# Hybrid attention: values evicted two steps late, masks two ahead, unread products on TensorE, first scores ahead of the last z half

## The chip, the cores and the metric

The kernel is one program on one core of a Trainium2 chip. The metric is the device time of the whole program in microseconds (us): the median of several executions. Beside the times there is one execution recorded by the hardware profiler. Engines are named as in the profile: PE (TensorE's matmuls), PEld (its weight loads, which overlap the matmuls), DVE (VectorE), ACT (ScalarE), POOL (GpSimd), and SP, which here only issues DMAs.

## What is computed

A long network on one sequence of 256 tokens of width 1024. First two blocks (a recurrent mixer with a feed-forward part, then differential attention with eight experts), then two layers of hybrid attention. The change touches only the last part, which in the reference is:

```python
def hybrid_layer(x, c, positions, ...):          # twice: l = 0, 1
    ...
    h = rms_norm_2(x, norm_g) * (1 + scale) + shift
    z = h @ w_in                                  # 1024 -> 2976
    c_q, c_kv, k_rope, g_mla, q_b, k_b, v_b, g_moba = jnp.split(z, ...)
    o_mla  = mla_attention(...)                   # 8 heads, q and k of width 96, v of 64, causal
    o_moba = moba_attention(...)                  # 8 heads of width 64, causal, with a bias by distance
    y = jnp.concatenate([silu(g_mla) * o_mla, silu(g_moba) * o_moba], -1) @ w_out
    return x + gate * y
```

With 256 tokens the blocks of moba are one block, so both attentions are a causal softmax over 256 keys.

## The kernel before

Every engine has its own instruction list, written out by hand; engines meet at semaphores. The eight PSUM banks are given out by a plan (`make_plan`, L162): each use of a bank has a name, an order, a bank and the engine that empties it ("a" ACT, "v" DVE, "e" the exponentials on ACT). `fill` on PE waits until the bank's use before has been emptied, `take` waits until PE has filled it, `wait_taken` waits until it has been emptied. DVE and ACT wait for each of their own instructions before the next one.

Large products run in fp32r as three passes (high times high, low times high, high times low; L1139 to L1141), from weights that ACT (`high`, L2824) and DVE (`low`, L1896) split into a high and a low part after their DMA. A half of a weight tile is one `high` and one `low`.

A hybrid layer on PE: the z chunks in the order 0, 2, 3, 4, 1, 5 (`by_token`, two halves j = 0, 1 each), between them small products and transposes. Between the halves of z chunk 5, `mla_heads` transposes the mla queries and keys (L1746). Then come 16 attention steps: i = 0 to 7 are moba, i = 8 to 15 mla; a step handles two heads (g) and one half of the queries (m = i mod 2), so even steps have 128 keys and odd ones 256. After the loop come the output products (`out_product`, L1803).

A step i passes over the engines like this:

- PE `scores(i)` (L1759; L1763 and L1764 for mla), into two alternating sets of banks by i mod 2. The bank for step i + 2 is free when ACT has finished `exponentials(i)`.
- DVE `masked(i)`: bias or mask (L2706, L2708), row maximum (L2711), for mla one tiny product more (L2714).
- ACT `exponentials(i)`: two activations, each followed by a read of the sum's accumulator (L3227).
- DVE `sums_inverted(i)`: one reciprocal (L2719), after the exponentials of i.
- PE `weights_transposed(i)`: 2 or 4 transposes (L1774), after the exponentials of i; ACT `weights_out(i)` copies them out (L3238).
- PE `values(i)`: the product with v (L1787); DVE `values_out(i)` scales it into O2 (L2726).

The orders of the three lists in the loop are: PE `scores(i+2)`, `weights_transposed(i)`, `values(i-1)`; DVE `masked(i+1)`, `sums_inverted(i)`, `values_out(i-1)`; ACT `exponentials(i+1)`, `weights_out(i)`. Into the loop are put: two `high` on ACT (after steps 2 and 3), two `low` on DVE (after steps 4 and 5), `heads_gated` (L2731) for the moba half on DVE after step 8, and at step 10 the transposes of that half on PE (`gated_to_channels`, L1797) with their copies on ACT (L2809) and DVE (L1916). A PE matmul of fp32 operands shows as two records, one of fp32r as one.

XTH is the fp32r tile that holds the high part of the layer's input during the z chunks and of the gated output later; its first two slices are next written after the loop.

Of the kernel before, what the change touches and what calls it, by code (L numbers as in the profile page):

```python
# [22 lines left out]
P = 128  # L23
# [100 lines left out]
class Plan:  # L124
# [7 lines left out]
    def add(self, name, who, bank=None):  # L132
        self.index[name] = len(self.by)
        self.bank.append(len(self.by) % 8 if bank is None else bank)
        self.by.append(who)
# [26 lines left out]
def make_plan():  # L162
# [141 lines left out]
    for l in range(DEPTH2):  # L304
        for u in range(4):
            add((("h", l), "xT", u), "v", 4 + u)

        def z_chunk(c):
            for m in range(TT):
                add(("z", l, c, m), "a" if c in (1, 5) else "av"[m], 2 * (Z_ORDER.index(c) % 2) + m)  # L310

        def pair_scores(i):
            for c in range(1 if i >= 8 else 2):
                add(("pair", l, "scores", i, c), "e", 2 * (i % 2) + c)

        z_chunk(0)
        if l == 0:
            for u in range(2):
                add(("mod_gate", 1, u), "v", 6 + u)
        z_chunk(2)  # L320
        for u in range(2):
            add(("cT", l, u), "a", 4 + u)
        z_chunk(3)
        for c in range(4):
            for m in range(TT):
                add(("up", l, c, m), "av"[m], 4 + (2 * c + m) % 4)
        z_chunk(4)
        z_chunk(1)
        for u in range(4):
            add(("mobaT", l, u), "av"[u % 2], 4 + u)  # L330
        for u in range(8):
            add(("mlaT", l, u), "av"[u % 2], 4 + u % 4)
        z_chunk(5)
        pair_scores(0)
        pair_scores(1)
        for i in range(17):
            if i < 14:
                pair_scores(i + 2)
            if i == 10:
                for u in (2, 3):  # L340
                    add(("yT", l, u), "v", 2 * u - 3)
            if i < 16:
                add(("pair", l, "weightsT", i), "a", 4 + i % 2)
            if i:
                add(("pair", l, "values", i - 1), "v", 6 + (i - 1) % 2)
        for u in range(2):
            add(("yT", l, u), "v", 4 + u)
        for c in range(2):
            for m in range(TT):
                add(("w_out", l, c, m), "v", 2 * m + 1 - c)  # L350
# [152 lines left out]
def build(nc, I, consts, buckets, out):  # L503
# [4 lines left out]
    with ctx:  # L508
# [155 lines left out]
        def fill(pe, name):  # L664

            i = PLAN.index[name]
            before = PLAN.emptied_before(i)
            if before is not None:
                pe.wait_ge(emptied[before[0]], before[1])
            return banks[PLAN.bank[i]]  # L670
# [6 lines left out]
        def wait_taken(eng, name):  # L677

            i = PLAN.index[name]
            who = PLAN.by[i]  # L680
            eng.wait_ge(emptied[who], sum(w == who for w in PLAN.by[:i + 1]))
# [422 lines left out]
        def _(pe):  # L1104
            mm = nc.tensor.matmul
# [405 lines left out]
            def scores(i):  # L1511

                h, m = DIFF_STEPS[i]
                w = (m + 1) * P
                qk = QKT[h // 4]
                b = [fill(pe, ("diff", "scores", i, c)) for c in range(2)]
                for c in range(2):
                    r = slice(64 * c, 64 * c + 64)
                    mm(b[c][:, 0:w], qk[r, h % 4, m * P:(m + 1) * P], qk[r, 4 + h % 4, 0:w],
                       start=True, stop=True).then_inc(filled, 1)  # L1520

            def weights_transposed(i):

                m = DIFF_STEPS[i][1]
                b = fill(pe, ("diff", "weightsT", i))
                pe.wait_ge(weights, i + 1)
                for k in range(m + 1):
                    last = nc.tensor.transpose(b[:, k * P:(k + 1) * P], AT[:, i % 2, k * P:(k + 1) * P], IDENT)
                last.then_inc(filled, 1)
# [204 lines left out]
            for l in range(DEPTH2):  # L1734
# [6 lines left out]
                def mla_heads(j):  # L1741

                    if j == 0:
                        return
                    pe.wait_ge(mla_ready, l + 1)
                    to_channels(("mlaT", l), 8, lambda u: [  # L1746
                        (96, (2 * i + m) * P, QK[:, m, (2 * u + i) * 96:(2 * u + i + 1) * 96])
                        for i in range(2) for m in range(TT)])

                def scores(i):  # L1750

# [12 lines left out]
                    mm(b[:, T:T + w], QKT2[0:96, 2 * g + 1, q], QKT2[0:96, 9 + 2 * g, 0:w],  # L1764
                       start=True, stop=True).then_inc(filled, 1)

                def weights_transposed(i):

                    m = PAIR_STEPS[i % 8][1]
                    b = fill(pe, ("pair", l, "weightsT", i))  # L1770
                    pe.wait_ge(exps, 16 + 16 * l + i + 1)
                    for c in range(2):
                        for k in range(m + 1):
                            last = nc.tensor.transpose(b[:, (2 * c + k) * P:(2 * c + k + 1) * P],  # L1774
                                                       EE2[:, i % 2, c, k * P:(k + 1) * P], IDENT)
                    last.then_inc(filled, 1)
# [62 lines left out]
                    (P, (2 * j + m) * P, ZB[:, m, ZQ + (2 * u + j) * P:ZQ + (2 * u + j + 1) * P])  # L1839
                    for j in range(2) for m in range(TT)])  # L1840
                z_chunk(5, mla_heads)
                wait_taken(pe, ("mobaT", l, 2))
                wait_taken(pe, ("mobaT", l, 3))
                scores(0)
                scores(1)
                for i in range(17):
                    if i == 6:
                        wait_taken(pe, ("mlaT", l, 6))
                        wait_taken(pe, ("mlaT", l, 7))
                    if i < 14:  # L1850
                        scores(i + 2)
                    if i == 10:
                        gated_to_channels((2, 3))
                    if i < 16:
                        weights_transposed(i)
                    if i:
                        values(i - 1)
                wait_taken(pe, ("yT", l, 3))
# [9 lines left out]
        def _(v):  # L1868
# [746 lines left out]
            for l in range(DEPTH2):  # L2615
# [112 lines left out]
                def heads_gated(at, z, c):  # L2728

                    wait_taken(v, ("z", l, c, 1))  # L2730
                    V(tt_(O2[:, :, at:at + 512], O2[:, :, at:at + 512], ZB[:, :, z:z + 512], MUL), o_ready)  # L2731
# [26 lines left out]
                for u in range(1, 8, 2):  # L2758
                    b = take(v, ("mlaT", l, u)).rearrange("p (g t) -> p g t", g=2)
                    V(ts(QKT2[0:96, 2 * u:2 * u + 2, :], b[0:96], prm("mla_columns", 2 * l + u // 4)[0:96], None, MUL), ev)  # L2760
                masked(0)
                for i in range(16):
                    if i < 15:
                        masked(i + 1)
                    sums_inverted(i)
                    if i == 10:
                        x_out(("yT", l), units=(2, 3))
                    if i:
                        values_out(i - 1)
                    if i in (4, 5):  # L2770
                        low()
                    elif i == 8:
                        heads_gated(512, ZGB, 5)
                values_out(15)
                heads_gated(0, ZG, 1)
                x_out(("yT", l), units=(0, 1))
# [555 lines left out]
```

## Time and profile before

| | us |
|---|---|
| median of 3 executions (2017.39 to 2021.28) | 2018.95 |
| the profiled execution | 2015.8 |
| its span, first to last instruction | 2014.0 |

The page of the profile gives busy time by engine, the span in 40 slices with the clock that was granted to TensorE (tenths of full speed; 1.0 is 2.4 GHz, 0.5 is 1.2 GHz), and the chain of work that ended last. The trace behind it can be asked for any stretch: busy time of each engine and the granted clock (windows), instructions in order of time (timeline), who waited for whom (waits), and the chain in order of time. In the timeline "[2.42 <-X]" says that the engine was idle for 2.42 us before the row, and what released it. Rows of one line that follow each other are merged: start, duration, and the count behind the shape. PE's matmuls are pipelined, so the cost of one is read from start to start, not from its duration.

The 16 steps of layer 0 lie between 1745.77 and 1802.42 us of the span, those of layer 1 between 1923.78 and 1983.19 us.

### The profile page before, as it was taken

To read this page: it belongs to the slowest core of one execution; us is meant where nothing else is said; L and a number is where in the kernel's file an instruction comes from. 1 tells how busy PE (TensorE), PEld (TensorE's weight loads), DVE (VectorE), ACT (ScalarE), POOL (GpSimd) and SP (SyncE) were. 2 spreads that over 40 slices of the span, in tenths; PEclk is the share of its full clock that TensorE was granted. 3 is DMA by queue.
4 is the path that set the end of the run, shared out by engine and by line. 5 is a ranking of instruction groups with operands and counts; after the bars stand their busy time and mean duration, and the time that the engine had idled before them with its cause. 6 is when DMAs were issued, how large, how long until landed. Compare 5 with 4: busy or idle time off the path is not lost.

```text
span 2014.0 us, 25785 instructions
## 1 busy us (share of the span) xinstructions
PE 1886.5 (94%) x9376; PEld 1580.4 (78%) x9376; DVE 1561.2 (78%) x1532; ACT 1163.4 (58%) x1218; POOL 59.8 (3%) x85
## 2 busy tenths in 40 slices
PE   7989999999877999999999999999999989888987
PEld 7888678887756788888888888888888877677766
DVE  5877768887674789898897888888888976656754
ACT  5632344435473667677676776686766755545452
POOL 2000011111100000000000000000000000000000
PEclk9999899999967999999999999999999999879968
DMA  6301269995412899999999999999999954214410
GB/s 222 126 1 43 80 239 318 332 308 176 136 42 106 298 380 331 374 347 362 371 339 371 350 361 368 341 372 347 363 345 358 378 175 152 84 43 138 153 62 22
DMA packets 161948, 489.03 MB, mean 243 GB/s; under 512 B 8178, under 2 KB 13427, under 8 KB 161744
## 3 DMA queue, kind: packets, MB, share of 16 engines
q1 hardware_dynamic: 153536, 458.21, 62.6%
q0 software_dynamic: 8336, 29.81, 4.2%
q8 instruction: 48, 0.79, 0.2%
q14 instruction: 28, 0.23, 0.0%
HBM read 485.36 MB, written 2.62 MB: 242 GB/s over the span
## 4 chain that ended last, share of the span: by engine, by line
PE 66%; DVE 14%; issue 10%; DMA 4%; ACT 4%; POOL 0%; DVEq 0%; ACTq 0%; POOLq 0%
PE bank L1139 19%; PE bank L1141 18%; PE bank L1140 18%; DVE weights_at L1896 4%; PE bank L1630 2%; DMA BIG<-in_e_ffn_down 2%; ACT weights_at L2824 2%; DVE BIG L2241 2%; PE bank L1348 1%; PE bank L1695 1%; PE bank L1336 1%; DMA BIG<-in_e_ffn_up 1%; DMA BIG<-in_e_w_in 1%; DMA BIG<-in_w_ada 1%; PE bank L1374 1%
## 5 line engine op out<-in xcount | busy, mean ns | idle before, releaser
L2482 DVE TENSOR_TENSOR expert_weights_low<-BIG,expert_weights_high 128x2048 fp32r<-128x2048 f32 x336 | 750.4, 2288 | 56.9 <-ACT expert_weights_high L3107 56.4
L3107 ACT ACTIVATE expert_weights_high<-BIG 128x2048 fp32r<-128x2048 f32 x336 | 625.0, 1922 | 65.1 <-DMA BIG<-in_o_moe_up 38.5
L1139 PE MATMUL bank<-expert_weights_high,expert_x_high 128*128 128x512 f32 x896 | 352.4, 393 | 2.4 <-DVE expert_x_low L2547 2.3
L1141 PE MATMUL bank<-expert_weights_low,expert_x_high 128*128 128x512 f32 x896 | 350.0, 391 | 0.0
L1140 PE MATMUL bank<-expert_weights_high,expert_x_low 128*128 128x512 f32 x896 | 349.7, 390 | 0.0
L1896 DVE TENSOR_TENSOR weights_at<-BIG,weights_at 128x2048 fp32r<-128x2048 f32 (+2 forms) x100 | 219.1, 2191 | 83.0 <-ACT weights_at L2824 80.9
L2824 ACT ACTIVATE weights_at<-BIG 128x2048 fp32r<-128x2048 f32 (+2 forms) x100 | 183.6, 1836 | 167.0 <-DMA BIG<-in_e_ffn_down 42.0
L1139 PE MATMUL bank<-weights_at,x_high 128*128 128x512 f32 (+2 forms) x608 | 244.9, 403 | 22.5 <-DVE weights_at L1896 8.3
L1140 PE MATMUL bank<-weights_at,x_low 128*128 128x512 f32 (+2 forms) x608 | 239.7, 394 | 0.0
L1141 PE MATMUL bank<-weights_at,x_high 128*128 128x512 f32 (+2 forms) x608 | 239.6, 394 | 0.0
L1139 PEld LDWEIGHTS bank<-expert_weights_high,expert_x_high 128*128 128x128 f32 x896 | 168.8, 188 | 36.8 <-DVE expert_x_low L2547 2.4
L1141 PEld LDWEIGHTS bank<-expert_weights_low,expert_x_high 128*128 128x128 f32 x896 | 168.5, 188 | 35.1
L1140 PEld LDWEIGHTS bank<-expert_weights_high,expert_x_low 128*128 128x128 f32 x896 | 168.8, 188 | 34.1
L1139 PE MATMUL bank<-expert_weights_high,expert_hidden_high 128*128 128x512 f32 x448 | 176.1, 393 | 0.0
L1141 PE MATMUL bank<-expert_weights_low,expert_hidden_high 128*128 128x512 f32 x448 | 174.7, 390 | 0.0
L1140 PE MATMUL bank<-expert_weights_high,expert_hidden_low 128*128 128x512 f32 x448 | 174.4, 389 | 0.0
L1139 PEld LDWEIGHTS bank<-weights_at,x_high 128*128 128x128 f32 x608 | 118.1, 194 | 50.3 <-issue 9.8
L1141 PEld LDWEIGHTS bank<-weights_at,x_high 128*128 128x128 f32 x608 | 117.4, 193 | 25.3
L1140 PEld LDWEIGHTS bank<-weights_at,x_low 128*128 128x128 f32 x608 | 118.1, 194 | 24.0 <-issue 0.5
L3154 ACT ACTIVATE expert_hidden_high<-bank 128x512 fp32r<-128x512 f32 x56 | 30.9, 596 | 168.8 <-PE bank L1695 168.8
L1141 PEld LDWEIGHTS bank<-expert_weights_low,expert_hidden_high 128*128 128x128 f32 x448 | 84.1, 188 | 17.8
L1140 PEld LDWEIGHTS bank<-expert_weights_high,expert_hidden_low 128*128 128x128 f32 x448 | 84.2, 188 | 17.1
(400 smaller groups left out, 2350.3 us busy)
## 6 DMA issues: line engine op xcount, KB each, us to landing
BIG<-in_o_moe_gate SPq DMA_DIRECT2D x112, 1024.0 KB, 5.1
BIG<-in_o_moe_up SPq DMA_DIRECT2D x112, 1024.0 KB, 5.3
BIG<-in_o_moe_down SPq DMA_DIRECT2D x112, 1024.0 KB, 5.0
BIG<-in_w_ada POOLq DMA_DIRECT2D x48, 512.0 KB, 4.8
BIG<-in_w_in SPq DMA_DIRECT2D x20, 1024.0 KB, 5.0
BIG<-in_o_w_qkv SPq DMA_DIRECT2D x12, 1024.0 KB, 5.0
BIG<-in_e_w_in SPq DMA_DIRECT2D x10, 1024.0 KB, 5.2
BIG<-in_e_ffn_gate SPq DMA_DIRECT2D x10, 1024.0 KB, 5.4
```

The source lines that it names most:

```text
L1139: mm(b, high_l, high_r, start=start, stop=False, skip_group_check=not check)
L1140: mm(b, low_l, high_r, start=False, stop=False, skip_group_check=not check)
L1141: last = mm(b, high_l, low_r, start=False, stop=stop, skip_group_check=not check)
L1336: last = mm(b[:, i * P:(i + 1) * P], AM[:, 4 * gr + i, :], YI[:, 4 * gr + i, :], start=True, stop=True)
L1348: last = mm(b[:, i * P:(i + 1) * P], lhs[:, k, :], rhs[:, k, :], start=True, stop=True)
L1630: last = mm(b[:, k * P:(k + 1) * P], XN[:, m, d * P:(d + 1) * P], PSEL[:, m, :], start=m == 0, stop=m == TT - 1)
L1896: V(tt_(WM[low_at][:, 0:n_], whole, WM[high_at][:, 0:n_].bitcast(F32), SUB), low_ready)
L2241: V(stt(ADAS[i], w_, s_cc[:, k:k + 1], ADAS[i], MUL, ADD), ada_used)
L2482: tt_(E_WL[q % E_SLOTS], half(q % E_SLOTS), E_WH[q % E_SLOTS].bitcast(F32), SUB).then_inc(w_low, 1)
L2824: A(f(WM[halves.pairs[g][0]][:, 0:whole.shape[1]], whole, ACT.Copy), high_ready)
L3107: f(E_WH[q % E_SLOTS], half(q % E_SLOTS), ACT.Copy).then_inc(w_high, 1)
L3154: f(E_HTH[:, h], b, ACT.Copy).then_inc(xh_high, 1)
```

## The change

Four things are changed, in both hybrid layers. On PE `scores(0)` moves from behind z chunk 5 to between its halves, after the transposes of mla (the plan's order moves with it). On PE a new function `opened(i, n)` takes the bank of step i's transposed weights and runs n fp32r products of 128 columns by 512 into it, which nothing reads and which the transposes overwrite: six at step 0, two at each of steps 1 to 15, ahead of `scores(i+2)`. On DVE `masked` runs two steps ahead instead of one and `values_out` two steps behind instead of one, and the order in a step becomes `values_out(i-2)`, `sums_inverted(i)`, `masked(i+2)`. On DVE `heads_gated` of the moba half goes from step 8 to the end of step 9, and at step 10 `x_out` goes to the end of the step. ACT's list is as before.

```diff
--- before.py
+++ after.py
@@ -330,8 +330,8 @@
             add(("mobaT", l, u), "av"[u % 2], 4 + u)
         for u in range(8):
             add(("mlaT", l, u), "av"[u % 2], 4 + u % 4)
+        pair_scores(0)
         z_chunk(5)
-        pair_scores(0)
         pair_scores(1)
         for i in range(17):
             if i < 14:
@@ -1746,6 +1746,9 @@
                     to_channels(("mlaT", l), 8, lambda u: [
                         (96, (2 * i + m) * P, QK[:, m, (2 * u + i) * 96:(2 * u + i + 1) * 96])
                         for i in range(2) for m in range(TT)])
+                    wait_taken(pe, ("mobaT", l, 2))
+                    wait_taken(pe, ("mobaT", l, 3))
+                    scores(0)
 
                 def scores(i):
 
@@ -1764,10 +1767,16 @@
                     mm(b[:, T:T + w], QKT2[0:96, 2 * g + 1, q], QKT2[0:96, 9 + 2 * g, 0:w],
                        start=True, stop=True).then_inc(filled, 1)
 
-                def weights_transposed(i):
+                def opened(i, full_products):
+
+                    b = fill(pe, ("pair", l, "weightsT", i))
+                    for _ in range(full_products):
+                        mm(b, XTH[:, 0, 0:P], XTH[:, 0:2, :], start=True, stop=True, skip_group_check=True)
+                    return b
+
+                def weights_transposed(i, b):
 
                     m = PAIR_STEPS[i % 8][1]
-                    b = fill(pe, ("pair", l, "weightsT", i))
                     pe.wait_ge(exps, 16 + 16 * l + i + 1)
                     for c in range(2):
                         for k in range(m + 1):
@@ -1839,20 +1848,19 @@
                     (P, (2 * j + m) * P, ZB[:, m, ZQ + (2 * u + j) * P:ZQ + (2 * u + j + 1) * P])
                     for j in range(2) for m in range(TT)])
                 z_chunk(5, mla_heads)
-                wait_taken(pe, ("mobaT", l, 2))
-                wait_taken(pe, ("mobaT", l, 3))
-                scores(0)
                 scores(1)
                 for i in range(17):
                     if i == 6:
                         wait_taken(pe, ("mlaT", l, 6))
                         wait_taken(pe, ("mlaT", l, 7))
+                    if i < 16:
+                        weights_bank = opened(i, 2 if i else 6)
                     if i < 14:
                         scores(i + 2)
                     if i == 10:
                         gated_to_channels((2, 3))
                     if i < 16:
-                        weights_transposed(i)
+                        weights_transposed(i, weights_bank)
                     if i:
                         values(i - 1)
                 wait_taken(pe, ("yT", l, 3))
@@ -2759,18 +2767,20 @@
                     b = take(v, ("mlaT", l, u)).rearrange("p (g t) -> p g t", g=2)
                     V(ts(QKT2[0:96, 2 * u:2 * u + 2, :], b[0:96], prm("mla_columns", 2 * l + u // 4)[0:96], None, MUL), ev)
                 masked(0)
+                masked(1)
                 for i in range(16):
-                    if i < 15:
-                        masked(i + 1)
+                    if i >= 2:
+                        values_out(i - 2)
                     sums_inverted(i)
-                    if i == 10:
-                        x_out(("yT", l), units=(2, 3))
-                    if i:
-                        values_out(i - 1)
+                    if i < 14:
+                        masked(i + 2)
                     if i in (4, 5):
                         low()
-                    elif i == 8:
+                    elif i == 9:
                         heads_gated(512, ZGB, 5)
+                    elif i == 10:
+                        x_out(("yT", l), units=(2, 3))
+                values_out(14)
                 values_out(15)
                 heads_gated(0, ZG, 1)
                 x_out(("yT", l), units=(0, 1))
```

## Rows read from the trace of the kernel before

**Rows 1.** The page: PE's busy time, and the granted clock in 40 slices.
```profile
PE 1886.5 (94%) x9376; PEld 1580.4 (78%) x9376; DVE 1561.2 (78%) x1532; ACT 1163.4 (58%) x1218; POOL 59.8 (3%) x85
PEclk9999899999967999999999999999999999879968
```

**Rows 2.** Windows, both stages: from:to, length, busy us by engine, clock, DMA share.
```profile
1745.77:1802.42 56.65, 44.42 (x217) 37.97 (x217) 32.47 (x76) 32.53 (x86) 0.00 (x0) 0.66 0.11 38
1923.78:1983.19 59.41, 45.63 (x217) 38.57 (x217) 32.44 (x76) 32.54 (x86) 0.00 (x0) 0.65 0.11 36
```

**Rows 3.** Waits in layer 0's stage: us in total, times, longest.
```profile
DVE BIG L2726 <- PE bank L1787: 16.1, 11, 3.3
ACT BIG L3227 <- DVE SM L2714: 7.8, 6, 2.0
```

**Rows 4.** The chain that ended last, in layer 1's stage, one turn: start, us.
```profile
1954.24 0.76 PE bank L1787 x4
1955.10 0.30 DVE BIG L2726
1955.42 0.44 DVE bank L2708
...
1956.86 0.66 ACT BIG L3227 x2
...
1958.30 0.83 PE bank L1763 x2
```

**Rows 5.** Windows around changes of the clock (columns as in rows 2), layer 0.
```profile
1747.40:1749.80 2.40, 0.00 (x0) 0.02 (x1) 1.47 (x3) 2.23 (x6) 0.00 (x0) 1.00 0.00 0
1751.10:1757.06 5.96, 5.96 (x26) 4.78 (x26) 2.23 (x6) 2.79 (x10) 0.00 (x0) 0.50 0.01 3
1774.00:1777.80 3.80, 3.80 (x17) 3.41 (x16) 0.66 (x2) 1.51 (x5) 0.00 (x0) 0.50 0.24 93
1781.00:1782.00 1.00, 1.00 (x7) 0.87 (x6) 0.90 (x4) 0.11 (x1) 0.00 (x0) 0.62 0.00 0
1788.10:1798.50 10.40, 7.12 (x48) 6.00 (x47) 7.22 (x22) 6.22 (x19) 0.00 (x0) 0.99 0.01 2
1736.60:1740.00 3.40, 3.40 (x34) 3.40 (x32) 2.02 (x3) 2.15 (x4) 0.00 (x0) 1.00 0.35 135
```

**Rows 6.** Windows of one pair of steps each: moba at half, mla at half, mla at full clock.
```profile
1932.03:1938.87 6.84, 6.04 (x27) 4.84 (x27) 3.48 (x10) 4.36 (x11) 0.00 (x0) 0.50 0.00 0
1946.76:1954.78 8.02, 6.68 (x26) 6.02 (x27) 4.79 (x9) 3.69 (x11) 0.00 (x0) 0.50 0.69 245
1791.35:1796.12 4.77, 3.85 (x27) 3.36 (x27) 2.74 (x10) 3.39 (x10) 0.00 (x0) 1.00 0.01 3
```

**Rows 7.** Timeline of PE: end of z chunk 5, first scores, first output products, layer 1.
```profile
1923.21 0.40 PE L1140 MATMUL bank<-weights_at,x_low 128*128 128x512 f32 x1
1923.45 0.40 PE L1141 MATMUL bank<-weights_at,x_high 128*128 128x512 f32 x1
1923.78 0.49 PE L1759 MATMUL bank<-BIG 64*128 64x128 f32 x4
1924.68 0.70 PE L1759 MATMUL bank<-BIG 64*128 64x256 f32 x4 [0.41 <-ACT BIG L3208]
1927.81 0.65 PE L1759 MATMUL bank<-BIG 64*128 64x128 f32 x4 [2.42 <-ACTq L3230]
...
1984.62 0.63 PE L1139 MATMUL bank<-weights_at,x_high 128*128 128x512 f32 x1
1985.05 0.63 PE L1140 MATMUL bank<-weights_at,x_low 128*128 128x512 f32 x1
```

**Rows 8.** Timelines of ACT and DVE, layer 1: table load, one high, one low.
```profile
1925.38 1.28 ACT L3227 ACT_TABLE_LOAD   x1 [0.84 <-DVE SM L2711]
...
1935.79 1.91 ACT L2824 ACTIVATE weights_at<-BIG 128x2048 fp32r<-128x2048 f32 x1
...
1942.32 2.29 DVE L1896 TENSOR_TENSOR weights_at<-BIG,weights_at 128x2048 fp32r<-128x2048 f32 x1
```

## The prediction, made before the changed kernel was run

> **What bounds the kernel now.** First the page: PE is busy 94% of the span, so time is to be had only where PE is late or slow, and the clock row shows where: the last two of its dips (slices 35 and 36, then 39 and 40) lie at and after the attention stages of the two hybrid layers [rows 1]. Then the windows of these stages: 56.65 and 59.41 us, PE busy for 44.4 and 45.6 of them, at a mean granted clock of 0.66 and 0.65 [rows 2]. So PE has work for about three quarters of the stage, and much of that runs at 1.2 GHz. Then the waits: the longest is DVE at `values_out`, 16.1 us in 11 waits for PE's `values`; ACT in turn waits 7.8 us for the tiny product that ends `masked` in the mla steps [rows 3]. The chain joins the two: `values(i-1)`, `values_out(i-1)`, mask and maximum of i + 2, exponentials of i + 2, then the next scores on PE [rows 4]. DVE stands at `values_out` while the scores that it is to mask next are there already. So the stage is a loop through all three engines in which none is full, and PE's idle time in it lowers the clock, which makes the loop longer.
>
> **DVE's order.** Afterwards `values_out(i-2)` stands ahead of `sums_inverted(i)`. `values(i-2)` on PE comes before `scores(i+1)`, so it is done by about the time that the exponentials of i end, and `sums_inverted(i)` and `masked(i+2)` need those anyway: the wait of 16.1 us has no successor at this place. What is late next is the loop exponentials(i), scores(i+2), mask(i+2), exponentials(i+2), two steps long. In the mla steps with 256 keys the chain gives 1.44 us for mask, maximum and their signal (1955.42 to 1956.86) and 1.44 for the exponentials and theirs (to 1958.30); the scores of one of the two heads take 0.83 there, mostly at the low clock [rows 4], so I take 1.0 for both at full clock and 0.2 for their signal: 4.1 us in two steps. Against it stand the engines' own sums. DVE: 32.47 less two `low` of 2.29 is 27.9, 3.5 us for each of the eight pairs of steps. ACT: 32.53 less the table load of 1.28 and two `high` of 1.91 is 27.4, or 3.4 a pair [rows 2, 8]. PE: 6.04 at half clock for a moba pair, so 3.0 at full, and 3.85 at full for an mla pair [rows 6].
>
> **The unread products.** An fp32r product of 512 columns costs 0.24 us at full clock (1923.21 to 1923.45) and 0.43 at half (1984.62 to 1985.05) [rows 7]; their weight loads overlap as those of all such products do. A layer has 36: 8.4 us of PE at full clock, 15.5 at half. A pair of steps gets four: PE then needs 4.0 us for a moba pair and 4.8 for an mla pair at full clock, and 7.8 and 8.4 at half. Below zero their direct cost can't go; what they can bring is the clock. At full clock PE becomes the fullest engine of the loop by about half a microsecond a pair. The bank that `opened(i)` takes was emptied by `weights_out(i-2)`, for which `values(i-2)` one step earlier has waited already: no new wait.
>
> **The clock.** It fell from 2.4 to 1.2 GHz after PE had stood still for 2.4 us at the loop's start (2.42 us, released by ACT's exponentials [rows 7]; the same in layer 0 [rows 5]). It rose again after 3.8 us without a gap, 1774.0 to 1777.8; it did not rise in 5.96 us without a gap, 1751.10 to 1757.06, so uninterrupted work is not by itself enough. It fell again at 1781 (0.62), after a gap of 1.3 us, and held at 0.99 for 10.4 us from 1788.1 with PE busy for 7.12 of them, 68% [rows 5]. With the products PE is busy for 80% and more of the stage at full clock (36 us of work in the 44 worked out below), and at half clock it has no gaps at all. I take from this that the clock is mostly 2.4 GHz, with one spell at 1.2 in each layer.
>
> PE's transposes are a point against it. The row: from 1736.6 to 1740.0 PE did nothing but transposes and the clock stayed at 1.00 [rows 5]. The Trainium skill, "TensorE: Matmul & The Clock Gate", Part 4: PE-mode transpose, says that a transpose doesn't count as PE being busy the way a matmul does. By that rule the stage would be worth less to the clock than its busy time says, and the second rival below would be what happens; by the row it would not.
>
> **First scores and the start.** `scores(0)` ahead of the last z half puts 0.35 to 0.5 us in front of that half (its two products take 0.49 us in the timeline [rows 7]; I take 0.42). It lets mask and maximum of step 0 be done early, so that ACT goes from its last z copy straight into the table load: the 0.84 us that it stood idle before the load go [rows 8]. Net -0.4 us a layer, between +0.5 and -0.9. From the last z product to the end of the first exponentials: z copy 0.9, table load 1.3, exponentials 0.9, so 3.1 us. `scores(1)` still waits for that z copy, and the six products (1.4 us) fill over half of the 2.42 us gap behind it.
>
> **The sum for one layer** at full clock, from placing the operations of the three lists one after the other with these durations, zero at the last z product: exponentials end at 3.1 (step 0), 6.0 (2), 11.6 (4), 17.0 (6), 23.1 (8), 26.9 (10), 32.9 (12), 37.8 (14) and 40.7 (15); the last transposes, copy and values take 2.6: 43.3. Of the 34.7 between steps 0 and 14, PE's own sum is four times 4.0 and three times 4.8, 30.4. The 4.3 more are what is not hidden of two `high` (3.8 on ACT, steps 2 and 3), two `low` (4.6 on DVE, steps 4 and 5) and step 10, where gate, transposes and copies follow each other on DVE, PE and ACT. Moved later by a step, gate and `x_out` cost between nothing and 1.2 us more than before, and lie in this sum. SP's loads of the last output weights wait for the two `low`, which come earlier; a load has the rest of the loop, over 20 us. With `scores(0)` 43.7. For one spell at half clock and for signals that I placed too tightly I add 2.3: 46.0 a layer, against 56.65 and 59.41. That is 116.1 less 92.0: **24 us**. Behind the loop the first eight output products run at half clock now (0.43 apart, layer 1 at 1984.6, against 0.24 [rows 7]); if the clock holds, 1.5 us a layer more, which I leave to the range.
>
> The profiled execution took 2015.8 us (span 2014.0); less 24 it would take 1991.8. The median of the runs shown is 3 us above it; I forecast the median: **1995 us**.
>
> **Rivals.**
>
> The period stays where full clock has it today. In the old order at 2.4 GHz the shortest pair took 4.8 us [rows 6], and the stretch from 1788.1 to 1798.5, some two pairs, gives 5.2 each [rows 5]. If semaphore latencies rather than the wait at `values_out` make that, the stage is 3.1 + 7 times 5.2 + 5 + 5.5 = 50, and the saving 116.1 - 100.8 = 15: 2004.
>
> The clock is mixed: a quarter of the stage at 1.2 GHz. All of it at half clock is PE's sum: four times 7.8, four times 8.4, six products, transposes of the gate, and 3.3 to start, near 73 us. A quarter of the way from 46 to 73 is 52.7: the saving is 11, 2008. For it: the fall at 1781 after only 1.3 us of gap. Against: nothing filled gaps then.
>
> Slower: the clock stays down. Then PE is the bound, and every step pays 0.86 us for two products that bring nothing. With the whole loop at 1.2 GHz the stages take 73 each, 30 us more than now: 2049. It decides at a stage of 58 us, that is with some 45% of the loop at half clock. For it: the 5.96 us without a gap and no rise. Against: the rises and the 10.4 us that held.
>
> The change doesn't do what it says: DVE's wait only moves to `sums_inverted`, because ACT's order (exponentials of i + 1 before the copy of i) was the bound all along, and the products fill the idle time. Then 2018 within 0.2%. Against: DVE's 16.1 us are waits for PE, not for ACT [rows 3].
>
> **How the numbers follow.** Forecast 0.58 (1986 to 2001, the low end with the output products and no spell at half clock), old period 0.16, mixed clock 0.13, slower 0.08, no effect 0.05. A measurement of this kernel tells about 0.2%, 4 us, from no change. Range 1985 to 2011: forecast and the first two rivals. Faster 0.87, same 0.05, slower 0.08.
>
> **What would show it.** Right: the wait of DVE at `values_out` for PE nearly gone; the mean clock of both stages over 0.9; no gap of PE over 2 us; a pair of mla steps in 4.6 to 5.0 us; stages of 43 to 49 us. Wrong: a clock near 0.5 with PE busy all through (slower); a clock of 1.0 and pairs of over 5.2 us (the old period); waits of the same size before `sums_inverted`; or a gap that opens behind the loop, so that a shorter stage doesn't shorten the span.

## Result and the profile after

The changed kernel takes 1984.0 us (median of four executions, 1983.4 to 1985.4) against 2018.3 for the kernel before (2017.4 to 2021.3): a ratio of 0.983, with an interval of 0.981 to 0.985. I had forecast 1995 with a range of 1985 to 2011. The sign and the direction of the mechanism were right. The saving, 34 us, was larger than the 24 I forecast, and the time lies 1 us below my range. Two executions in the series below, one of the kernel before and one of the early split, ran at a mean clock of 0.55 and 0.60 and took 3129 and 3173 us; they stand in no ratio.

The page of the changed kernel, lines as in [rows 1]:

```profile
PE 1872.3 (94%) x9448; PEld 1564.1 (79%) x9448; DVE 1561.3 (79%) x1532; ACT 1164.6 (59%) x1218; POOL 59.9 (3%) x85
PEclk9999899999967899999999999999999999999999
```

PE has 72 matmuls more and is busy 14 us less. The two dips at the attention stages (slices 35, 36, 39 and 40 in [rows 1]) are gone.

The two stages as windows, from the start of the last z product to the first output product (columns as in [rows 2]), and three more windows of the same kernel behind them: layer 1's one spell at a lower clock, and two places at the change of layers.

```profile
1744.93:1787.59 42.66, 37.25 (x251) 29.66 (x249) 31.59 (x74) 32.59 (x86) 0.00 (x0) 1.00 0.15 50
1909.55:1952.30 42.75, 38.44 (x251) 31.30 (x249) 31.60 (x74) 32.58 (x86) 0.00 (x0) 0.96 0.15 50
1926.00:1931.00 5.00, 5.00 (x28) 4.66 (x27) 4.53 (x6) 2.91 (x10) 0.00 (x0) 0.66 0.63 211
1815.00:1819.00 4.00, 2.62 (x12) 2.62 (x13) 0.57 (x2) 0.42 (x1) 0.61 (x1) 0.50 0.84 260
1891.00:1895.00 4.00, 2.14 (x5) 1.79 (x6) 3.97 (x2) 0.00 (x0) 0.00 (x0) 0.73 0.25 57
```

[Rows 2] count from the instruction behind that z product, 0.33 us later (1923.45 and 1923.78 in [rows 7]); from its start the stages before took 56.98 and 59.74. All stages below are counted from its start. So the stages became 14.3 and 17.0 us shorter, 31.3 together, and the granted clock rose from 0.66 and 0.65 to 1.00 and 0.96. The whole span went from 2014.0 to 1981.8, 32.2 less. The difference between that and the stages is small: 0.5 gained ahead of the first stage, 0.9 lost between the stages (121.03 to 121.96 us), 1.3 gained behind the second (30.8 to 29.5). The medians differ by 34.3, since the profiled execution of before (2015.8) lay 2.5 below its median.

Four of the waits in layer 0's stage (engine, line, whom it waits for: us in total, times, longest), in the order of the list; rows between them are left out at the dots:

```profile
DVE bank L2714 <- PE bank L1762: 8.6, 6, 6.1
...
ACT BIG L3237 <- DVE SM L2722: 3.5, 4, 2.3
...
DVE BIG L2734 <- PE bank L1796: 1.9, 3, 1.2
...
DVE SM L2727 <- ACT BIG L3237: 0.4, 2, 0.2
```

Lines have moved: `values_out` is L2734 now (L2726 before), `values` L1796, the mask L2714, the exponentials L3237, `sums_inverted` L2727. DVE's wait at `values_out` went from 16.1 us in 11 waits [rows 3] to 1.9 in 3. It didn't move to `sums_inverted` (0.4). ACT's wait for the tiny product ahead of the mla exponentials went from 7.8 to 3.5. DVE's 8.6 us at the mask have one wait of 6.1 in them: that is the start of the stage, where the scores of step 1 stand behind the last z half.

What bounds the loop now can be read from the chain that ended last. One turn of the mla half of layer 1, its longest pieces (start, us, engine, line):

```profile
1940.50 0.84 PE bank L1796 x8
1941.34 0.52 PE bank L1774 x2
1941.86 0.43 PE bank L1766 x2
1942.29 0.43 PE bank L1767 x2
1942.72 0.44 PE bank L1783 x4
```

In [rows 4] the same turn ran PE, DVE, DVE, ACT, PE. Now all of this turn is PE: values, the two unread products (L1774), scores, transposes, each right behind the one before. In the moba half the chain still goes through ACT, and two pieces of it are its `high`, 1.9 us each:

```profile
1916.73 0.57 ACT BIG L3237 x2
1917.33 0.57 ACT BIG L3237 x2
...
1918.49 1.92 ACT weights_at L2834
1920.43 0.47 ACT BIG L3237 x2
1920.92 0.47 ACT BIG L3237 x2
1921.55 0.61 ACT BIG L3248
...
1922.18 1.92 ACT weights_at L2834
```

### The profile page after: what moved, and what is told of

Read it like the earlier page. It is cut to its first block, busy times and chain, and to the rows that moved or that the text cites. A ratio compares the mean times of both kernels' runs of the same rounds, so it can differ in the third digit from the quotient of the medians.

```text
span 1981.8 us, 25897 instructions
## 1 busy us (share of the span) xinstructions
PE 1872.3 (94%) x9448; PEld 1564.1 (79%) x9448; DVE 1561.3 (79%) x1532; ACT 1164.6 (59%) x1218; POOL 59.9 (3%) x85
## 4 chain that ended last, share of the span: by engine, by line
PE 75%; DVE 9%; issue 9%; ACT 3%; DMA 2%; POOL 0%; DVEq 0%; POOLq 0%; ACTq 0%
PE bank L1139 21%; PE bank L1141 21%; PE bank L1140 21%; PE bank L1630 2%; PE bank L1348 2%; DVE weights_at L1904 1%; PE bank L1695 1%; ACT weights_at L2834 1%; PE bank L1336 1%; DMA BIG<-in_e_ffn_gate 1%; PE bank L1433 1%; PE bank L1374 1%; DVE x_low L1931 1%; DMA BIG<-in_e_ffn_up 0%; PE bank L1126 0%
```

## Experiments

The result alone can't say which part did it: DVE's order, the products and `scores(0)` came together, and the clock rose with them. The first four kernels take the change apart. The kernels that follow ask what the clock was worth, how many products are best, what the loop is made of, and whether the two `high` and `low` that stand on the new chain can go elsewhere.

I compare stages from the traces, one profiled execution of each kernel, and not whole times alone: these carry up to 8 us from work ahead of the stage. With the same instructions ahead of it, the last z product of the first stage started anywhere between 1744.9 us (the changed kernel) and 1753.5 (the kernel with one product a step). Each pair of rows below is layer 0 and layer 1, with columns as in [rows 2].

### The change taken apart

**DVE's order alone.** The kernel before, with only the new list on DVE:

```diff
                 masked(0)
+                masked(1)
                 for i in range(16):
-                    if i < 15:
-                        masked(i + 1)
+                    if i >= 2:
+                        values_out(i - 2)
                     sums_inverted(i)
-                    if i:
-                        values_out(i - 1)
+                    if i < 14:
+                        masked(i + 2)
...
+                values_out(14)
                 values_out(15)
```

> Only DVE's order is changed (masks two ahead, values evicted two late, gate and x_out at their new places); no unread products, scores(0) behind z chunk 5 as before. Theory A (order and products are both needed: the order opens the loop, the products keep the clock at 2.4 GHz): the 2.4 us gap of PE at the loop's start is still there, the clock falls, and PE at 1.2 GHz with 6.0 to 6.7 us of work a pair becomes the bound: stages of about 50 us, 16 us saved, 2002 (1996 to 2008), mean clock 0.6 to 0.8. Rival B (the order alone gives it, the products only fill idle time): stages of 43, 1984 to 1988. Rival C (the clock alone gives it): 2016 to 2019.

**The products alone.** DVE's list and `scores(0)` as before, two unread products a step and six at the start on PE:

```diff
+                    if i < 16:
+                        weights_bank = opened(i, 2 if i else 6)
                     if i < 14:
                         scores(i + 2)
```

> Only the unread products are added (six, then two a step); DVE's order and scores(0) as before. Theory A: the clock holds at over 0.9, but the loop through values_out stays, at 4.8 to 5.2 us a pair: stages of about 50 us, 2000 (1994 to 2008). Rival B: the products stand on the path at a low clock and bring nothing: 2018 to 2030. Rival C: 1984 to 1990.

**All but the products.** The changed kernel with none of them:

```diff
-                        weights_bank = opened(i, 2 if i else 6)
+                        weights_bank = opened(i, 0)
```

> The changed kernel without any unread product: new DVE order and scores(0) ahead of the last z half. Theory A: PE stands still for about 1.7 us at the start and again at the two highs and lows; the clock falls for part of the stage: 1990 to 2002, mean clock 0.65 to 0.9. Rival B: 1982 to 1986. Rival C: 2015 to 2018.

**First scores alone.** As the last, and DVE's list as before; of the change only `scores(0)` ahead of the last z half is left:

> Only scores(0) goes ahead of the last z half; DVE's order as before, no products. Theory A, by the prediction's sum: exponentials of step 0 about 0.4 us earlier a layer, 0.8 us in all, so 2017 to 2018; the clock falls at the start as before. Rival: the shorter gap of PE at the start (about 1.7 instead of 2.4 us) keeps the clock up in the first steps: 2005 to 2014.

The stages, in this order (order alone, products alone, all but the products, first scores alone):

```profile
1750.41:1795.71 45.30, 38.08 (x218) 32.03 (x217) 32.46 (x76) 32.57 (x86) 0.00 (x0) 0.77 0.14 47
1915.48:1960.94 45.46, 38.37 (x218) 31.83 (x217) 32.46 (x76) 32.58 (x86) 0.00 (x0) 0.77 0.15 47
...
1743.93:1800.00 56.07, 45.17 (x254) 35.51 (x253) 32.45 (x76) 32.59 (x86) 0.00 (x0) 0.85 0.12 38
1924.14:1980.41 56.27, 45.23 (x254) 35.67 (x253) 32.45 (x76) 32.57 (x86) 0.00 (x0) 0.85 0.11 38
...
1745.02:1789.35 44.33, 36.02 (x214) 30.31 (x213) 31.60 (x74) 32.58 (x86) 0.00 (x0) 0.81 0.15 48
1909.76:1953.52 43.76, 32.67 (x214) 27.24 (x213) 31.61 (x74) 32.57 (x86) 0.00 (x0) 0.88 0.15 49
...
1750.88:1810.79 59.91, 49.77 (x214) 42.91 (x213) 31.59 (x74) 32.54 (x86) 0.00 (x0) 0.57 0.10 36
1932.75:1989.22 56.47, 44.08 (x214) 37.63 (x213) 31.59 (x74) 32.53 (x86) 0.00 (x0) 0.66 0.12 38
```

Both layers together: before 116.7, order alone 90.8, products alone 112.3, all but the products 88.1, first scores alone 116.4, the changed kernel 85.4. The order by itself brings 26.0 of the 31.3 us, at a clock of only 0.77. The products by themselves bring the clock to 0.85, higher than the order does, and the stage stays at 56: 4.4 us. Read down the clock column against the lengths: a stage of 56 at 0.85 and one of 45 at 0.77 can't both be explained by the clock. Neither single kernel came out as I had expected: the order alone took less than the 50 us I had put on it and more than the 43, and the products alone took more than 50, at a clock below 0.9.

The wait says why. At `values_out`, layer 0, first with the order alone, then with the products alone:

```profile
DVE BIG L2726 <- PE bank L1787: 3.8, 5, 1.3
...
DVE BIG L2733 <- PE bank L1792: 15.2, 10, 3.3
```

With the products alone PE is faster, and DVE stands at the same wait nearly as long as before (15.2 us against 16.1).

The order has parts that no kernel here takes apart: the masks two ahead, the values two behind, and the new places of gate and `x_out`. One wait of before prices the last of them. It stands at `x_out` in step 10, once a layer, and with the order alone it is gone:

```profile
DVE x_low L1916 <- ACT x_high L2809: 2.1, 1, 2.1
```

If all of it was on the path, it is 2.1 us of the 11.7 and 14.3 that the order brings in the two layers; the wait at `values_out` fell by 12.3 in layer 0. How the rest divides between the masks and the values is not shown.

On top of the order, the products are worth 2.7 us for both layers (88.1 to 85.4), `scores(0)` 2.7 as well (90.8 to 88.1), but `scores(0)` pays for a part of that ahead of the stage. PE's timeline there, before and then after:

```profile
1736.58 3.66 PE L1171 MATMUL bank<-CST,BIG 128*96 128x128 f32 x32
1739.99 0.48 PE L1139 MATMUL bank<-weights_at,x_high 128*128 128x512 f32 x1
...
1735.47 3.66 PE L1171 MATMUL bank<-CST,BIG 128*96 128x128 f32 x32
1739.06 0.49 PE L1762 MATMUL bank<-BIG 64*128 64x128 f32 x4
1739.48 0.50 PE L1139 MATMUL bank<-weights_at,x_high 128*128 128x512 f32 x1
```

From the transposes to the last z half it is 3.41 us before and 4.01 after, 0.60 more a layer. That leaves 1.5 us of the 2.7, and in the changed kernel 0.2 a layer at the start: the first exponentials end 0.8 earlier behind the last z product (3.35 us against 4.18), less the 0.60 ahead of it. I had put it at 0.4. By itself, in the old order, it brings nothing that can be told from no change.

The ratios of whole times are: order alone 0.987 (interval 0.983 to 0.991), products alone 0.996 (0.994 to 0.998), all but the products 0.989 (0.985 to 0.993), first scores alone 0.999 (0.998 to 1.001). They rank as the stages do, but for one: by the stages "all but the products" should lie below the order alone; it lies above, and the intervals overlap. Its whole times run from 1984.9 to 2002.9, and its profile is of the shortest of them. Two of its six executions took 1985, at a mean clock of 0.964 over the whole program; four took 1996 to 2003, at 0.949 to 0.952. The nine of the changed kernel had 0.961 to 0.968. So the 2.7 us for the products hold for profiled executions. By the ratios (0.989 against 0.983, and 0.984 when the changed kernel was run again) they are worth 10 to 12 us, and products and first scores together 7 to 9 counted from the order alone. What the longer executions lost and where, no trace here shows; that stays open. The order stays the largest part either way: 0.987 is some 25 us of the 32 to 35.

### How many products

The changed kernel again, beside three other numbers of products: six at the start only, one a step, four a step. Each of the three kernels has one of the added lines.

```diff
-                        weights_bank = opened(i, 2 if i else 6)
+                        weights_bank = opened(i, 0 if i else 6)   # six at the start only
+                        weights_bank = opened(i, 1 if i else 6)   # one a step
+                        weights_bank = opened(i, 4 if i else 6)   # four a step
```

> The changed kernel itself, beside the three variants of it in this call. Theory A: with its order and its products the clock has no spell that costs anything, so its executions lie close together: 1983 to 1987, spread under 5 us, where the variant without products spread over 18. Rival (the first four executions were lucky, the clock falls in some): a spread of 10 us and more.

> The changed kernel with the six products at step 0 only and none later. Theory A (both the start and the gaps at the two highs and lows can lower the clock): the fall at the start goes, a fall in the middle is left in some executions: 1983 to 1996, spread of 8 us or more. Rival (the start gap alone lowers the clock): 1979 to 1983, spread under 5.

> The changed kernel with one unread product a step instead of two (six at step 0 as before). Theory A: PE has 0.47 us less a pair; where PE was the fullest engine the loop gets faster by up to 1 us a layer, and PE's gaps get longer by as much. If one product a step still holds the clock: 1982 to 1984; if it falls in part: 1986 to 1996 with a wide spread. Rival (the products after the start do nothing for the clock): 1980 to 1983.

> The changed kernel with four unread products a step from step 1 on instead of two (six at step 0 as before): 30 more a layer, 7.0 us of PE at 2.4 GHz. Theory A (PE is the fullest engine of the new loop, with 37 of 42.7 us): PE's gaps take 2 to 3 us of it, the rest is on the path: stages of 46 to 48 us, clock 1.00. Rival (another engine or the signals set the new loop): 43 to 44 us.

The stages in this order:

```profile
1748.93:1791.56 42.63, 37.23 (x251) 29.66 (x249) 31.61 (x74) 32.58 (x86) 0.00 (x0) 1.00 0.15 50
1913.53:1956.30 42.77, 38.47 (x250) 31.29 (x249) 31.61 (x74) 32.58 (x86) 0.00 (x0) 0.96 0.15 50
...
1748.99:1792.76 43.77, 35.68 (x220) 30.06 (x219) 31.60 (x74) 32.58 (x86) 0.00 (x0) 0.84 0.16 49
1913.18:1956.94 43.76, 34.43 (x221) 28.83 (x219) 31.60 (x74) 32.57 (x86) 0.00 (x0) 0.88 0.15 49
...
1753.53:1798.24 44.71, 38.50 (x236) 31.37 (x234) 31.60 (x74) 32.58 (x86) 0.00 (x0) 0.89 0.14 48
1918.62:1961.60 42.98, 36.80 (x236) 29.52 (x234) 31.60 (x74) 32.58 (x86) 0.00 (x0) 0.92 0.15 50
...
1749.20:1795.11 45.91, 43.45 (x281) 35.33 (x279) 31.60 (x74) 32.56 (x86) 0.00 (x0) 1.00 0.13 47
1917.05:1962.93 45.88, 43.46 (x281) 35.34 (x279) 31.60 (x74) 32.55 (x86) 0.00 (x0) 1.00 0.14 47
```

The changed kernel's stages repeat within 0.03 us. Its whole times were 1986.4 to 1992.1 this time, a spread of 5.6 us where I had expected under 5; with six at the start they spread over 9, with one a step over 12. With none, six, one, two and four products the two layers take 88.1, 87.5, 87.7, 85.4 and 91.8 us, at mean clocks of 0.85, 0.86, 0.90, 0.98 and 1.00. Two is the best of these. Once the clock stands at 1.00 more products only cost: 30 more at 0.23 us are 7 us of PE a layer, of which 3.2 lengthen the stage; the rest falls into idle time. And without any, the clock is far from bad: PE then has some 30 us of full-speed work (37.3 in the changed kernel less 8.4 for the products) in a stage of 44, and spells at half clock fall in part into its idle time. In whole times six at the start, one a step and two a step can't be told apart (0.984 for each, with about 0.0025 on either side); only the traces show a difference, of one execution each. The kernel with four a step has a single execution.

### Is the loop through `values_out` the bound?

If DVE's place in the loop set the old stage, more time on DVE at `values_out` lengthens it nearly in full, and less in the new order. So `values_out` writes its result twice, in the kernel before and in the changed one:

```diff
+                    V(tt_(v3(O2[:, m, at:at + P], 2), v3(b, 2), bc(s_rcb[:, i % 2, :], 2, [P, 2, 64]), MUL))
                     V(tt_(v3(O2[:, m, at:at + P], 2), v3(b, 2), bc(s_rcb[:, i % 2, :], 2, [P, 2, 64]), MUL), ev)
```

> The kernel before, with values_out done twice in each step of both layers (the same values written again, 0.32 us of DVE more a step, 5.1 us a layer; the bank is released after the second). Theory A' (after the first runs: in the old order the loop values_out, mask, exponentials, scores, transposes, values sets the stage, whatever the clock): nearly all of it is on the path: stages of 61 to 63 us against 57.0 and 59.7, with DVE's wait for PE at values_out no shorter. Rival (the low clock of PE sets the stage): hidden in DVE's 16 us of waiting: 57 to 60 us.

> The changed kernel with values_out done twice in each step, as in the run beside it. Theory A': values_out is off the loop now; DVE has 29.7 us of work in 42.7, and 5.1 more are hidden but for the steps with the two lows and the gate: stages of 43 to 45 us. Rival (DVE is the bound of the new loop): 47 to 48 us.

There is one execution of each.

```profile
1742.12:1804.78 62.66, 51.18 (x218) 43.37 (x217) 36.82 (x91) 32.53 (x86) 0.00 (x0) 0.57 0.11 34
1926.28:1988.30 62.02, 47.54 (x218) 40.20 (x217) 36.82 (x91) 32.54 (x86) 0.00 (x0) 0.62 0.10 35
...
1747.29:1792.60 45.31, 40.59 (x251) 32.41 (x249) 35.97 (x89) 32.59 (x86) 0.00 (x0) 0.92 0.13 47
1914.56:1959.89 45.33, 40.63 (x250) 32.40 (x249) 35.98 (x89) 32.60 (x86) 0.00 (x0) 0.92 0.13 47
```

DVE is busy 4.4 us more in each stage. The old order pays 5.7 and 2.3 us for it (8.0 of 8.7, at a clock of 0.57 and 0.62 instead of 0.66 and 0.65), the new one 2.7 and 2.6 (5.2 of 8.8, at 0.92 instead of 0.98). The difference has the right sign and is smaller than I expected (45.3 us lies just above my 43 to 45): in the new order DVE has less to spare than I thought. By itself this pair of kernels would not settle it; the kernels with order alone and products alone do.

### A better version

The chain of the changed kernel goes through two `high` on ACT in steps 2 and 3, and DVE's two `low` in steps 4 and 5 stand between masks. ACT and DVE have waits at the start of the stage (ACT one of 2.2 us for the last z product, DVE one of 6.1). So the first half of the output weights is split there, and the second in step 3 (`high`) and 5 (`low`) in one kernel, in steps 11 and 13 in the other:

```diff
+                high()                       # ACT, ahead of its copies of z chunk 5
                 z_out(5)
...
-                    if i in (2, 3):
+                    if i == 3:               # i == 11 in the second kernel
                         high()
...
                 masked(0)
+                low()                        # DVE
                 masked(1)
...
-                    if i in (4, 5):
+                    if i == 5:               # i == 13 in the second kernel
                         low()
```

> The changed kernel with one of the two highs on ACT moved out of the loop to ahead of its copies of z chunk 5, and one of the two lows on DVE to behind masked(0), where the trace shows both engines waiting for PE. Theory A (placement): a high of 1.9 us and a low of 2.3 are on the loop's path, with 0.5 to 1 us of slack each; about 3 us a layer less, 1976 to 1980. Rival (they are hidden behind PE): 1983 to 1985; or the longer ACT and DVE queues delay the last z half: 1986.

> The changed kernel with the first high and low ahead of the loop as in the run early_split, and the second high moved from step 3 to step 11 on ACT, the second low from step 5 to step 13 on DVE, into the mla steps, where PE needs 4.8 us a pair and ACT and DVE about 3.4. Theory A: each is then hidden behind PE but for half a microsecond: stages of 39 to 40 us against 42.7 of the changed kernel and 41.1 of early_split, clock 1.00; the whole 1977 to 1983 on this chip. Rival (a high or low delays the loop by its length wherever it stands): stages of 41 us; or the second load of the output weights, which waits for that low, comes too late: a wait of ACT for a DMA behind the loop.

```profile
1751.86:1792.94 41.08, 37.05 (x250) 29.59 (x249) 29.31 (x73) 30.64 (x85) 0.00 (x0) 1.00 0.15 52
1913.32:1954.40 41.08, 37.08 (x251) 29.61 (x249) 29.30 (x73) 30.63 (x85) 0.00 (x0) 1.00 0.16 52
...
1749.78:1790.09 40.31, 36.81 (x250) 29.65 (x249) 29.30 (x73) 30.67 (x85) 0.00 (x0) 1.00 0.09 28
1910.54:1950.86 40.32, 36.82 (x251) 29.66 (x249) 29.31 (x73) 30.67 (x85) 0.00 (x0) 1.00 0.10 29
```

Both stages take 41.1 us with the early split and 40.3 with the late one, against 42.7. The first half, moved to the start, is worth 1.6 us a layer where I had expected 3: in layer 1's chain one `high` is gone, but the `low` of step 5, which was not on it before, now stands there with 2.3 us, and PE is busy for 37.1 of the 41.1 us. Its whole times, 1978.1 to 1988.2 with a median of 1983.9, lie in the range I had given for no gain, not at 1976 to 1980. The second half, moved to the mla steps, is worth 0.8 more; I had expected a stage of 39 to 40, and its `high` and `low` are on the chain there too (1.9 and 2.3 us). I had feared for its late load; the stretch between the stages didn't grow (120.5 us against 122.0 in both executions of the changed kernel). The late version takes 1982.1 us, 0.9805 of the kernel before (0.979 to 0.982), the lowest ratio of all kernels here (the early split has 0.981). Against the changed kernel that is 0.2 to 0.3%, about what can be told from no change in whole times; the 2.4 us a layer stand in the traces.

## Why the prediction was right and wrong

**The placement was right.** The middle of the sum was a list of the times at which the exponentials end, zero at the last z product, at full clock. Measured in layer 0 of the changed kernel from the end of the reads of the sum's accumulator, behind 1744.93:

| step | 0 | 2 | 4 | 6 | 8 | 10 | 12 | 14 | 15 | first output product |
|---|---|---|---|---|---|---|---|---|---|---|
| forecast | 3.1 | 6.0 | 11.6 | 17.0 | 23.1 | 26.9 | 32.9 | 37.8 | 40.7 | 43.3 |
| after | 3.4 | 6.2 | 11.8 | 17.3 | 23.4 | 27.2 | 33.0 | 37.7 | 40.2 | 42.7 |
| before | 4.2 | 6.9 | 15.2 | 23.1 | 29.5 | 37.6 | 45.8 | 50.5 | 53.2 | 57.0 |

No step is off by more than 0.3 us up to step 14, and the end by 0.6. DVE's wait, the clock over 0.9, no gap of PE over 2 us (the longest is 1.59) and mla pairs of 4.8 us (from step 8 to 14, 14.3 in three pairs; singly 3.9, 5.8 with the gate in it, and 4.7) are as I had written. Two details were not: `values(i-2)` stands behind `scores(i+1)` in PE's list, not before it, and what DVE still waits for it is the 1.9 us above; and 36 products at 0.24 us are 8.6, not 8.4, which they are at the 0.23 that the changed kernel shows.

**The step that failed is the allowance.** I added 2.3 us a layer "for one spell at half clock and for signals that I placed too tightly". Neither cost anything like it. The signals were placed well. A spell came in layer 1 alone, 5 us at a clock of 0.66 (the third window of the first table), and it cost at most 0.1: the stage is 42.75 against 42.66 in layer 0, which had none (with the late split, where neither layer has one, the two take 40.32 and 40.31). PE comes out of it 1.6 us later than in layer 0 (the unread products at 1930.61 below are at 1764.37 there, counted from each stage's start), but a wait of 1.1 us that PE has in layer 0 soon after is gone in layer 1, and the exponentials of steps 6 to 10 end at the same times in both. In the terms of the forecast the 31.3 of the stages exceed 24.0 by 7.3:

- 4.6 from the allowance, twice 2.3;
- 1.2 from the placement's end, twice 43.3 against 85.4;
- 0.8 from `scores(0)`, which I added to the stage with 0.42 a layer; it lies ahead of it, with 0.60;
- 0.7 from the zero. The forecast says only "at the last z product"; read as its start, as in the table, it lies 0.33 a layer ahead of the start of [rows 2]. Read as the instruction behind it, this item is nothing and the one on the placement 1.9.

Only the first of these was a judgement; the others are bookkeeping, and all four went the same way. From 1995 to 1984.0 it is 11.0 us: these 7.3, then 2.8 because I added 3.2 from the profiled execution to the median and 0.4 was right, then 0.9 outside the stages. So the allowance alone would not have put the time outside the range; that all the errors went one way was bad luck. The 1.5 us a layer that I left to the range for the output products came behind layer 1 (1.3 in the tail; they are 0.23 apart now, not 0.43 as in [rows 7]). Behind layer 0 they did not show in the sum: at the change of layers the clock is 0.50 and 0.73 for 4 us each (the last two windows of the first table), where before had only the first of the two (0.57 for 4 us), and the stretch between the stages became 0.9 longer.

**The clock was priced too high as a cause.** I wrote that PE's idle time lowers the clock, "which makes the loop longer", and treated the order and the products as one repair of both. The order alone takes the stage from 57 and 60 to 45 at 0.77; the products alone take the clock to 0.85 and leave the stage at 56. The pieces of the chain that ended last, added up over layer 1's stage, say why (the chain reaches back to that stage only). Before, 28.4 us of it are PE and 28.1 ACT and DVE, one after the other. With the products alone it is 22.1 and 31.1: PE's part became shorter, 2.2 of it are the unread products themselves, and the part of ACT and DVE stayed, whose work doesn't change with PE's clock (DVE is busy for 31.6 us in the stage at 0.57 and in the one at 1.00). With the order alone it is 26.1 and 17.4, and with all but the products, at a clock of 0.88, 12.1 and 28.1 in a stage of 43.8: in the new order the two parts run side by side, and the stage is nearly as long whichever of them the chain names. Nor does the mean clock of a stage give its length where the list is the same: before, 0.66 and 0.65 go with 56.98 and 59.74 us, and with the first scores alone 0.66 and 0.57 with 56.47 and 59.91. What the full clock would bring in the old order without unread products, no run shows. What I took for two repairs was 26.0 us for the one and, in the profiled executions, 2.7 on top of it for the other.

**The rivals were priced by the wrong row.** "The old period at full clock" I put at a stage of 50, from pairs of 4.8 and 5.2 us late in the loop [rows 5, 6]. The kernel with products alone is close to that case (0.85), and it took 56. By the ends of its exponentials in layer 0 its seven pairs took 2.8, 7.0, 7.0, 7.3, 9.2, 7.2 and 5.0 us: pairs with `high`, `low` and the gate in them cost more, one ran in part at half clock, and I had taken the cheap ones for all seven. "Slower", with the whole loop at half clock, would have needed the products to bring no clock at all; in the old order they raised it by 0.2. "Mixed clock" did not happen, at 1.00 and 0.96. "No effect" fell with the wait at `sums_inverted`, 0.4 us.

**The clock after the change.** DVE's list by itself took the granted clock from 0.66 and 0.65 to 0.77 with not one matmul added. The Trainium skill, "TensorE: Matmul & The Clock Gate", section "Loop structure matters more than you think", says that the loop nest decides whether the matmuls stay warm. The traces agree. They show besides that the clock doesn't rank the gains: the products alone took it to 0.85 and saved 4.4 us, the list alone saved 26.0.

What stays open: why layer 1 falls to half clock and layer 0 doesn't (below), and the spread of the whole times without products.

## What to carry to other kernels

When several engines wait on each other and none is full, look for the engine that stands in order at a wait while the input of its next operation is there already; swapping these two in its list was worth 26 of 31 us here, with the clock still at 0.77. A low granted clock in such a stage is as likely a sign of the idle time as its cause: undo one at a time before paying for warm-up work, and count that work as a cost as soon as its engine is on the chain (in the profiled executions two products a step won 2.7 us, and four lost 6.4 against two). And where operations are placed one after the other with durations from the trace, as was done here, take the sum as it is, and put doubts into the range rather than into the middle.

## What the runs showed of the hardware

The clock doesn't follow from the gap ahead of it alone. Both layers of the changed kernel run the same list, and both have a gap of 1.59 us on PE ahead of the scores of the same step (timeline; the idle time ahead in brackets):

```profile
1760.86 0.70 PE L1762 MATMUL bank<-BIG 64*128 64x256 f32 x4 [1.59 <-ACTq L3240]
...
1925.48 0.70 PE L1762 MATMUL bank<-BIG 64*128 64x256 f32 x4 [1.59 <-ACTq L3240]
1926.97 1.20 PE L1774 MATMUL bank<-x_high 128*128 128x512 f32 x2
1930.61 0.70 PE L1774 MATMUL bank<-x_high 128*128 128x512 f32 x2
```

Behind the first the clock stayed at 1.00; behind the second the pair of unread products took 1.20 us where it takes 0.70 at full clock, and 4 us later it was back. The changed kernel run again gave the same two clocks for the stages, 1.00 and 0.96. And the price of a spell isn't its length: 5 us at 0.66 cost 0.1 us here.
